# First modulation of a two-layer trunk: its last quarter of 512 channels computed as two parts of 256

## Chip, cores and metric

The kernel runs on one core of a Trainium2 chip. The metric is the device time of one execution in microseconds (us), as the median of several runs.

## The reference, cut to what matters

Two layers act on x, 256 tokens of 2048 channels. Each layer starts with a modulation: a vector c of 2048 values is multiplied with w_ada, and the shift and scale it gives are applied to the normalised x. The result h goes into one large product with w_in, whose columns feed three branches (a gated delta rule, a gated convolution, a sparse attention).

```python
cond = jax.nn.silu(c)
for layer in range(DEPTH):
    shift, scale, gate = jnp.split((cond @ w_ada[layer] + b_ada[layer])[:, None, :], 3, axis=-1)
    h = rms_norm(x, norm_g[layer]) * (1.0 + scale) + shift
    (qkv_a, z_a, beta_raw, alpha_raw, glu_in, z_b, q_c, k_c, v_c, z_c,
     q_i, k_i, w_i, gate_raw) = split_columns(h @ w_in[layer])
    ...
```

The change touches only layer 0's shift and scale, h, and the first three of the four groups of 512 columns of glu_in.

## The kernel before

**Layout.** Channels lie on the 128 partitions: 2048 channels are 16 tiles "kt" of 128, and a tile of h is 128 channels by 256 tokens. All is float32. Each product is made of three matmuls on rounded parts (high x high, high x low, low x high; function `three`, L940 to L942), so h exists as ah (high) and al (low), and a weight chunk as wh and wl.

**Weight chunks.** w_in comes in chunks of 2 kt by 512 columns (512 KB), through a ring of four slots. SyncE requests a chunk into raw once the chunk four before is split (`stream`, L394); ScalarE rounds it to wh once it has landed and TensorE has used the chunk four before (`rounds`, L560); GpSimd writes wl = raw - wh (L539); TensorE uses it in 2 x 4 x 3 = 24 matmuls and counts w_used. Below, "chunk n" is the n-th of these in the program.

**The first modulation.** To have h early, layer 0 computes shift and scale in four quarters of 512 channels. For a quarter, SyncE requests eight loads of w_ada (`ada_load`, L370; each is two transfers of 512 KB, for shift and for scale, two kt each), through four slots adaw. "Load n" counts them, 0 to 31; load n waits until load n - 4 is used (ada_used). VectorE adds up the 16 kt, one step of 128x1024 each, in `ada_part` (L1427, L1429), partly in PSUM and partly in acc. TensorE turns the totals onto partitions with one-column matmuls (`ada_sum`, L1029). VectorE makes mods and gsc of them (`quarter_mods`, L1483, L1487), then xs = merged * gsc + mods (L1526); ScalarE makes the high halves ah (`h_high`, L600), and VectorE the low ones (`h_low`, L1502), two kt at a time. Between these, VectorE adds the first steps of the next quarter (ADA_SIDE) and normalises x (L1412).

**The order of the work.** Every engine's order is written out by hand; semaphores join them. TensorE takes for each quarter the 4 kt of three column groups, called pairs 0, 1 and 2 (`part_gemm`), two chunks a pair, 24 chunks in all: chunks 18 to 23 belong to the last quarter. Each pair's PSUM keeps its sum through all quarters. Then it takes the fourth group (pair 3) with chunks 24 to 31, all 16 kt, and after that five more groups. SyncE mixes the chunks among the loads: chunks 18 to 23 are requested after load 31, then the masks (L361), eight skew stores (L430), then chunk 24 on. ScalarE casts chunk 18, makes h_high(3), and casts chunks 19 to 23. When the pairs are done, it copies pair 0 to glt (L623), takes the tanh of pair 1 (L548) and copies pair 2 to glt1 (L629); VectorE then starts the depthwise convolution (L1568, L1570).

The order in TensorE's block:

```python
for q in range(4):
    ada_sum(q)
    for pair in range(3):
        part_gemm(hc, pair, H, 4 * q, 4, G_IN, paired=pair == 0)
        hc += 2
part_gemm(hc, 3, H, 0, KT, G_IN)
```

## Time and profile before

| | us |
|---|---|
| median of 3 runs | 2204.05 (2202.7 to 2205.69) |
| the profiled execution, its own time | 2206.72 |
| its span in the profile | 2204.9 |
| TensorE busy, matmuls | 2140.4 (97%) |
| GpSimd busy | 1664.8 (76%) |
| VectorE busy | 1225.2 (56%) |
| ScalarE busy | 959.7 (44%) |

The profile is of one execution. A timeline row gives start, duration, engine, line, what is written from what, the form, how often, and in brackets the idle time before it with what ended it. Matmul ends are modelled: at the upper clock matmuls follow each other at 0.12 us although each is shown as 0.28. PE is TensorE, PEld its weight load, DVE VectorE, ACT ScalarE, POOL GpSimd, SP SyncE. PEclk is the granted TensorE clock as a share of 2.4 GHz.

### The profile page before, as it was taken

The page shows a single profiled execution, that of the slowest core. Times are in us where ns is not written, and L with a number is a line of the kernel's source. Part 1 is how long each engine was busy: PE and PEld are TensorE (multiplying, and loading weights), DVE is VectorE, ACT ScalarE, POOL GpSimd, SP SyncE. Part 2 cuts the span into 40 slices and gives each one's busy share as a digit, 9 for nine tenths or more (in the row PEclk, how much of TensorE's full clock was granted, in tenths as well). Part 3 has the DMA queues.
Part 4 walks back from the last instruction along what each step waited for, and adds up shares of the span by engine and source line. Part 5 has one row for each costly group of instructions (what it writes and reads, how often), then busy time and mean ns, then how long its engine had stood idle before and what let it go on. Part 6 is the DMA issues. An engine that isn't in the chain of part 4 may idle for free.

```text
span 2204.9 us, 37807 instructions
## 1 busy us (share of the span) xinstructions
PE 2140.4 (97%) x14842; PEld 1949.9 (88%) x14842; DVE 1225.2 (56%) x2153; ACT 959.7 (44%) x1056; POOL 1664.8 (76%) x676
## 2 busy tenths in 40 slices
PE   5799999999999999999989999999999999999999
PEld 3789999988879988788989999999788998888899
DVE  6859974847655455544562894756667455430110
ACT  3334444483333544444344344446633354444442
POOL 1558858767765898998868886877667679998876
PEclk7889999999999999999999999999999999999999
DMA  9978646545553699898975775555545458966754
GB/s 363 382 266 233 182 126 183 162 138 159 158 157 115 218 353 340 295 340 310 350 256 172 195 211 147 170 163 150 156 148 158 133 182 306 350 206 202 223 192 153
DMA packets 228987, 479.59 MB, mean 218 GB/s; under 512 B 22096, under 2 KB 26448, under 8 KB 220272
## 3 DMA queue, kind: packets, MB, share of 16 engines
q1 hardware_dynamic: 228688, 477.54, 67.1%
q8 instruction: 96, 1.57, 0.3%
q14 instruction: 43, 0.35, 0.0%
q10 hardware_dynamic: 160, 0.13, 0.0%
HBM read 471.19 MB, written 6.29 MB: 217 GB/s over the span
## 4 chain that ended last, share of the span: by engine, by line
PE 42%; POOL 30%; issue 23%; DVE 3%; ACT 1%; DVEq 1%; POOLq 0%; ACTq 0%
POOL wl L539 30%; PE ps L940 13%; PE ps L941 13%; PE ps L942 13%; DVE score L1632 1%; PE ps L1302 0%; ACT wh L560 0%; POOLq L538 0%; PE ps L1309 0%; PE ps L1290 0%; PE ps L1236 0%; ACTq L737 0%; PE ps L1225 0%; PE ps L1258 0%; PE ps L1252 0%
## 5 line engine op out<-in xcount | busy, mean ns | idle before, releaser
L539 POOL TENSOR_TENSOR wl<-raw,wh 128x1024 fp32r<-128x1024 f32 x672 | 1664.6, 2491 | 527.1 <-ACT wh L560 525.4
L560 ACT CAST wh<-raw 128x1024 fp32r<-128x1024 f32 x672 | 703.8, 1050 | 1118.2 <-PE ps L942 871.9
L940 PE MATMUL ps<-ah,wh 128*128 128x256 f32 x3008 | 867.7, 288 | 24.1 <-DVE al L1502 14.9
L941 PE MATMUL ps<-al,wh 128*128 128x256 f32 x3008 | 856.5, 285 | 0.0
L942 PE MATMUL ps<-ah,wl 128*128 128x256 f32 x3008 | 856.1, 285 | 0.0
L940 PEld LDWEIGHTS ps<-ah,wh 128*128 128x128 f32 x3008 | 583.0, 194 | 30.5 <-DVE al L1502 15.2
L941 PEld LDWEIGHTS ps<-al,wh 128*128 128x128 f32 x3008 | 583.2, 194 | 3.9 <-issue 3.6
L942 PEld LDWEIGHTS ps<-ah,wl 128*128 128x128 f32 x3008 | 582.8, 194 | 0.0
L940 PE MATMUL ps<-wh,ah 128*128 128x512 f32 (+1 forms) x832 | 319.8, 384 | 0.9 <-POOL wl L539 0.9
L942 PE MATMUL ps<-wh,al 128*128 128x512 f32 (+1 forms) x832 | 317.1, 381 | 0.0
L941 PE MATMUL ps<-wl,ah 128*128 128x512 f32 (+1 forms) x832 | 317.0, 381 | 0.0
L1570 DVE SCALAR_TENSOR_TENSOR ps<-upad,par,ps 128x256 f32<-128x256 f32 x480 | 199.7, 484 | 8.9
L940 PEld LDWEIGHTS ps<-wh,ah 128*128 128x128 f32 x832 | 156.5, 188 | 31.2 <-POOL wl L539 1.3
L942 PEld LDWEIGHTS ps<-wh,al 128*128 128x128 f32 x832 | 156.4, 188 | 30.4
L941 PEld LDWEIGHTS ps<-wl,ah 128*128 128x128 f32 x832 | 156.5, 188 | 28.9
L1448 DVE SCALAR_TENSOR_TENSOR ps<-modw,cond,ps 128x2048 f32<-128x2048 f32 x49 | 115.4, 2355 | 113.8 <-DMA modw<-w_ada 111.0
L940 PE MATMUL ps<-wh,yh 128*128 128x512 f32 x384 | 153.9, 401 | 0.0
L942 PE MATMUL ps<-wh,yl 128*128 128x512 f32 x384 | 149.8, 390 | 0.0
L941 PE MATMUL ps<-wl,yh 128*128 128x512 f32 x384 | 149.8, 390 | 0.0
L1736 DVE TENSOR_TENSOR ps<-ps,gbias 128x1024 f32<-128x1024 f32 x24 | 29.6, 1233 | 130.5 <-PE ps L942 130.5
L940 PEld LDWEIGHTS ps<-wh,yh 128*128 128x128 f32 x384 | 72.0, 188 | 16.1 <-POOL wl L539 0.7
L942 PEld LDWEIGHTS ps<-wh,yl 128*128 128x128 f32 x384 | 72.1, 188 | 15.5
(280 smaller groups left out, 1702.7 us busy)
## 6 DMA issues: line engine op xcount, KB each, us to landing
raw<-w_in SPq DMA_DIRECT2D x512, 512.0 KB, 3.7
modw<-w_ada SPq DMA_DIRECT2D x64, 1024.0 KB, 7.8
adaw<-w_ada SPq DMA_DIRECT2D x64, 512.0 KB, 8.5
raw<-w_out SPq DMA_DIRECT2D x64, 512.0 KB, 5.2
raw<-w_pc SPq DMA_DIRECT2D x32, 512.0 KB, 3.8
raw<-w_pb SPq DMA_DIRECT2D x32, 512.0 KB, 6.3
raw<-w_pa SPq DMA_DIRECT2D x32, 512.0 KB, 4.8
gbias<-b_gate SPq DMA_DIRECT2D x24, 256.0 KB, 4.3
```

The lines of the kernel that those rows point to most:

```text
L539: nc.gpsimd.tensor_tensor(wl[:, s], raw[:, s], wh[:, s].bitcast(F32), ALU.subtract).then_inc(sem("w_split"), 1)
L560: A.copy(wh[:, s], raw[:, s]).then_inc(sem("w_rounded"), 1)
L940: M.matmul(o, lh, rh, start=start, stop=False, skip_group_check=True)
L941: M.matmul(o, lh, rr, start=False, stop=False, skip_group_check=True)
L942: return M.matmul(o, ll, rh, start=False, stop=last, skip_group_check=True)
L1448: unit = V.scalar_tensor_tensor(o, w, cond[:, kt:kt + 1], wide if first < kt <= last else side, ALU.mult, ALU.add)
L1570: V.scalar_tensor_tensor(o, upad[:, ct, back:back + T], w, o, ALU.mult, ALU.add)
L1632: V.scalar_tensor_tensor(sc, rl[:, h, 0:keys], tok[:, qb, h:h + 1], sc, ALU.mult, ALU.add)
L1736: V.tensor_tensor(ps[:, 0:2, :], ps[:, 0:2, :], spread(gbias[:], 1, [P, TT, GW]), ALU.add).then_inc(sem("gate_sum"), 1)
```

## The change

The last quarter becomes two parts of 2 kt (256 channels). Each part has its own loads, totals, turning matmuls, mods, high and low halves, and its own three pieces of the pairs. So the program has five parts (ADA_PARTS).

- A load of the last quarter holds 4 kt by 256 columns instead of 2 kt by 512. Loads 24 to 27 are the first part's and 28 to 31 the second's. The bytes are the same; a contiguous row in memory is 1 KB instead of 2 KB.
- VectorE adds 16 steps of 128x512 for each part, up to the last step in one PSUM bank (pb[3]), with 3 steps of the first part and 4 of the second taken ahead (ADA_AHEAD).
- Chunks 18 to 23 come in another order: (pair 0, pair 1, pair 2) for kt 12 and 13, then the same for kt 14 and 15.
- TensorE turns the first part's totals ahead of pair 2 of the third quarter, and the second part's ahead of pair 2 of the first part.
- ScalarE casts chunks 18 and 19, makes the first part's high halves, casts 20 and 21, makes the second's, casts 22 and 23. Its copies of the pairs move by one or two casts.

```diff
         ADA_SIDE = 2
+        ADA_PARTS = ((0, 4), (4, 4), (8, 4), (12, 2), (14, 2))
+        ADA_AHEAD = (0, ADA_SIDE, ADA_SIDE, 3, 4)
         NORM = (2, 0, 1, 3)
...
+        def by_eighth(slot):
+            return adaw[slot][:].rearrange("p m s n -> p (m s n)").rearrange("p (m s n) -> p m s n", m=4, s=2)
         block = ctx.enter_context(nc.Block())
...
                 for part in (SHIFT, SCALE):
-                    col = part * D + q * GW
-                    sp.dma_start(adaw[j % 4][:, :, part], wa[0, :, 2 * j:2 * j + 2, col:col + GW]
-                                 ).then_inc(ada_landed[j % 4], 16)
+                    if q < 3:
+                        col = part * D + q * GW
+                        sp.dma_start(adaw[j % 4][:, :, part], wa[0, :, 2 * j:2 * j + 2, col:col + GW]
+                                     ).then_inc(ada_landed[j % 4], 16)
+                    else:
+                        col = part * D + 3 * GW + j // 4 * T
+                        sp.dma_start(by_eighth(j % 4)[:, :, part], wa[0, :, 4 * (j % 4):4 * (j % 4) + 4, col:col + T]
+                                     ).then_inc(ada_landed[j % 4], 16)
                 if n == 2:
...
-                    chunks = [(col, j) for q in range(4) for col in (first, second, first + GW)
-                              for j in range(2 * q, 2 * q + 2)]
+                    chunks = [(col, j) for k0, k in ADA_PARTS for col in (first, second, first + GW)
+                              for j in range(k0 // HK, (k0 + k) // HK)]
...
                     act.wait_ge(sem("gsc_ready"), q + 1)
-                    for kt in range(4 * q, 4 * q + 4):
+                    for kt in range(ADA_PARTS[q][0], sum(ADA_PARTS[q])):
                         last = A.activation(ah[:, kt], merged[:, kt], ACT.Identity, bias=mods[:, kt:kt + 1],
...
                         hc += 6
-                    rounds(hc, 1, hc % RING)
+                    rounds(hc, 2, hc % RING)
                     h_high(3)
-                    rounds(hc + 1, 5, (hc + 1) % RING)
+                    rounds(hc + 2, 2, (hc + 2) % RING)
+                    h_high(4)
+                    rounds(hc + 4, 2, (hc + 4) % RING)
                     hc += 6
-                    act.wait_ge(sem("w_used"), hc)
-                    A.copy(glt[:], pairv(0)).then_inc(gemm_free[0], 1)
                     rounds(hc, 2)
                     act.wait_ge(sem("w_used"), hc + 2)
+                    A.copy(glt[:], pairv(0)).then_inc(gemm_free[0], 1)
+                    rounds(hc + 2, 1, 2)
+                    act.wait_ge(sem("w_used"), hc + 3)
                     tanh_half(pairv(1), pairv(1)).then_inc(sem("glt_ready"), 1)
-                    rounds(hc + 2, 2, 2)
+                    rounds(hc + 3, 1, 3)
                     act.wait_ge(sem("w_used"), hc + RING)
...
                 for part in (SHIFT, SCALE):
-                    for j in range(4 * q, 4 * q + 4):
+                    for j in range(ADA_PARTS[q][0], sum(ADA_PARTS[q])):
                         mm = M.matmul(pb[2][:, part * KT + j:part * KT + j + 1], acc[:, part, j * P:(j + 1) * P],
...
                     pe.wait_ge(sem("bias_row"), HEADS)
-                    for q in range(4):
-                        ada_sum(q)
+                    for q, (k0, k) in enumerate(ADA_PARTS):
+                        if q < 3:
+                            ada_sum(q)
                         for pair in range(3):
-                            part_gemm(hc, pair, H, 4 * q, 4, G_IN, paired=pair == 0)
-                            hc += 2
+                            if q in (2, 3) and pair == 2:
+                                ada_sum(q + 1)
+                            part_gemm(hc, pair, H, k0, k, G_IN, paired=pair == 0)
+                            hc += k // HK
                     part_gemm(hc, 3, H, 0, KT, G_IN)
...
-                wide, side = ps[:, 6:8, :], acc[:, :, q * GW:(q + 1) * GW]
+                first, width = ADA_PARTS[q]
+                wide, side = ps[:, 6:8, :], acc[:, :, first * P:(first + width) * P]
+                if q > 2:
+                    wide = pb[3].rearrange("p (s n) -> p s n", s=2)
                 V.drain()
                 for kt in range(k0, k1):
-                    j, m = kt // 2, kt % 2
+                    j, m = kt // (8 // width), kt % (8 // width)
                     if m == 0:
-                        dve.wait_ge(ada_landed[j % 4], 32 * ((8 * q + j) // 4 + 1))
-                    w = adaw[j % 4][:, m]
-                    ahead = ADA_SIDE if q else 0
+                        dve.wait_ge(ada_landed[j % 4], 32 * ((first * 2 + j) // 4 + 1))
+                    w = by_eighth(j)[:, m] if q > 2 else adaw[j % 4][:, m]
+                    ahead = 0 if q > 2 else ADA_AHEAD[q]
                     o = wide if ahead <= kt < KT - 1 else side
...
                                                    ALU.mult, ALU.add)
-                    if m:
+                    if m == 8 // width - 1:
                         u.then_inc(sem("ada_used"), 1)
...
-                part = slice(4 * q, 4 * q + 4)
+                k0, k = ADA_PARTS[q]
                 dve.wait_ge(sem("ada_turned"), q + 1)
                 for n in (SHIFT, SCALE):
-                    at = n * KT + 4 * q
-                    last = V.tensor_tensor(mods[:, at:at + 4], pb[2][:, at:at + 4], p_(0, "b_ada", at, 4), ALU.add)
-                if q == 3:
+                    at = n * KT + k0
+                    last = V.tensor_tensor(mods[:, at:at + k], pb[2][:, at:at + k], p_(0, "b_ada", at, k), ALU.add)
+                if q == 4:
                     last.then_inc(sem("mods_ready"), 1)
                 V.drain()
-                V.scalar_tensor_tensor(gsc[:, part], mods[:, KT + 4 * q:KT + 4 * q + 4], 1.0,
-                                       p_(0, "norm_g", 4 * q, 4), ALU.add, ALU.mult)
+                V.scalar_tensor_tensor(gsc[:, k0:k0 + k], mods[:, KT + k0:KT + k0 + k], 1.0,
+                                       p_(0, "norm_g", k0, k), ALU.add, ALU.mult)
                 done("gsc_ready")
...
                 if layer == 0:
-                    for q in range(4):
+                    for q, (k0, k) in enumerate(ADA_PARTS):
                         if q == 0:
...
                             normed_x()
-                        normed_quarter(q)
-                        ada_part(q, ADA_SIDE + 1 if q else 10, KT)
+                        if q < 4:
+                            normed_quarter(q)
+                        ada_part(q, ADA_AHEAD[q] + 1 if q else 10, KT)
                         if q == 0:
...
                             dve.wait_ge(sem("con_landed"), 16)
-                        if q < 3:
-                            ada_part(q + 1, 0, ADA_SIDE)
+                        if q < 4:
+                            ada_part(q + 1, 0, ADA_AHEAD[q + 1])
                         quarter_mods(q)
-                        for kt in range(4 * q, 4 * q + 4):
+                        for kt in range(k0, k0 + k):
                             V.tensor_scalar(xs[:, kt], merged[:, kt], gsc[:, kt:kt + 1], mods[:, kt:kt + 1],
...
                         V.drain()
-                        h_low(2 * q)
-                        h_low(2 * q + 1)
-                        if q < 3:
-                            ada_part(q + 1, ADA_SIDE, ADA_SIDE + 1)
+                        for n in range(k0 // 2, (k0 + k) // 2):
+                            h_low(n)
+                        if q < 4:
+                            ada_part(q + 1, ADA_AHEAD[q + 1], ADA_AHEAD[q + 1] + 1)
```

How the instructions move. ScalarE, from the cast of chunk 16 (slot 0; the number behind raw_landed is the chunk's number modulo 4) to the glt copy, before:

```order
L560 CAST wh<-raw 128x1024 [waits w_used,raw_landed0]
L560 CAST wh<-raw 128x1024 [waits w_used,raw_landed1]
L560 CAST wh<-raw 128x1024 [waits w_used,raw_landed2]
L600 ACTIVATE ah<-merged,mods,gsc 128x256 [waits gsc_ready]
L600 ACTIVATE ah<-merged,mods,gsc 128x256 x3
L560 CAST wh<-raw 128x1024 [waits w_used,raw_landed3]
L560 CAST wh<-raw 128x1024 [waits w_used,raw_landed0]
L560 CAST wh<-raw 128x1024 [waits w_used,raw_landed1]
L560 CAST wh<-raw 128x1024 [waits w_used,raw_landed2]
L560 CAST wh<-raw 128x1024 [waits w_used,raw_landed3]
L623 COPY glt<-ps 128x1024 [waits w_used]
```

and in the change:

```order
L571 CAST wh<-raw 128x1024 [waits w_used,raw_landed0]
L571 CAST wh<-raw 128x1024 [waits w_used,raw_landed1]
L571 CAST wh<-raw 128x1024 [waits w_used,raw_landed2]
L571 CAST wh<-raw 128x1024 [waits w_used,raw_landed3]
L611 ACTIVATE ah<-merged,mods,gsc 128x256 [waits gsc_ready]
L611 ACTIVATE ah<-merged,mods,gsc 128x256
L571 CAST wh<-raw 128x1024 [waits w_used,raw_landed0]
L571 CAST wh<-raw 128x1024 [waits w_used,raw_landed1]
L611 ACTIVATE ah<-merged,mods,gsc 128x256 [waits gsc_ready]
L611 ACTIVATE ah<-merged,mods,gsc 128x256
L571 CAST wh<-raw 128x1024 [waits w_used,raw_landed2]
L571 CAST wh<-raw 128x1024 [waits w_used,raw_landed3]
```

The high halves of the last quarter (L600, now L611) stood behind chunk 18's cast and ahead of chunk 19's; now the first part's two stand behind chunk 19's cast, and the second part's two behind chunk 21's.

TensorE, at the turning of the last quarter's totals (ps<-con,acc), before:

```order
L942 MATMUL ps<-ah,wl 128x256
L940 MATMUL ps<-ah,wh 128x256
L941 MATMUL ps<-al,wh 128x256
L942 MATMUL ps<-ah,wl 128x256
L1029 MATMUL ps<-con,acc 128x1 [waits ada_summed]
L1029 MATMUL ps<-con,acc 128x1 x7
L940 MATMUL ps<-ah,wh 128x256 [waits w_split,hT_ready]
L941 MATMUL ps<-al,wh 128x256
```

and in the change, at the turning of the first part's, between pairs 1 and 2 of the third quarter:

```order
L956 MATMUL ps<-ah,wl 128x256
L954 MATMUL ps<-ah,wh 128x256
L955 MATMUL ps<-al,wh 128x256
L956 MATMUL ps<-ah,wl 128x256
L1043 MATMUL ps<-con,acc 128x1 [waits ada_summed]
L1043 MATMUL ps<-con,acc 128x1 x3
L954 MATMUL ps<-ah,wh 128x256 [waits w_split]
L955 MATMUL ps<-al,wh 128x256
```

The turning stood between two quarters, ahead of a matmul that waits for hT_ready too; now four matmuls of it (the rows count a turning matmul once; the trace has two records for each) stand ahead of pair 2, inside the third quarter. Those of the second part stand in the same way inside the first part, with 96 other matmuls between the two places.

## Rows read from the trace of the kernel before

**Rows 1.** The page, busy time, share and instructions of each engine.

```profile
PE 2140.4 (97%) x14842; PEld 1949.9 (88%) x14842; DVE 1225.2 (56%) x2153; ACT 959.7 (44%) x1056; POOL 1664.8 (76%) x676
```

**Rows 2.** Waits, whole run: us in total, times, longest us.

```profile
PE ps L940 <- POOL wl L539: 4.8, 4, 2.3
```

**Rows 3.** Timeline, TensorE, start, us, line, then idle before and releaser.

```profile
129.99 2.16 PE L1029 MATMUL ps<-con,acc 128*128 128x1 f32 x16 [1.15 <-DVEq L1433]
135.01 0.58 PE L940 MATMUL ps<-ah,wh 128*128 128x256 f32 x1 [2.86 <-DVE al L1502]
...
153.75 0.28 PE L942 MATMUL ps<-ah,wl 128*128 128x256 f32 x1
155.30 0.39 PE L940 MATMUL ps<-ah,wh 128*128 128x256 f32 x1 [1.28 <-POOL wl L539]
```

**Rows 4.** Timeline, ScalarE, 127 to 144 us.

```profile
127.51 1.05 ACT L560 CAST wh<-raw 128x1024 fp32r<-128x1024 f32 x1 [9.04 <-DMA raw<-w_in]
132.75 2.07 ACT L600 ACTIVATE ah<-merged,mods,gsc 128x256 fp32r<-128x256 f32 x4 [4.18 <-DVEq L1385]
134.72 2.92 ACT L560 CAST wh<-raw 128x1024 fp32r<-128x1024 f32 x3
139.72 1.05 ACT L560 CAST wh<-raw 128x1024 fp32r<-128x1024 f32 x1 [2.07 <-PE ps L942]
142.60 1.05 ACT L560 CAST wh<-raw 128x1024 fp32r<-128x1024 f32 x1 [1.83 <-PE ps L942]
```

**Rows 5.** Busy us by stretch (PE, PEld, DVE, ACT, POOL), PEclk, DMA share, GB/s.

```profile
136.00:138.00 2.00, 2.00 (x12) 2.00 (x11) 0.00 (x0) 1.65 (x2) 2.00 (x1) 0.50 0.00 0
```

**Rows 6.** SyncE's requests in its timeline, and the first four of the six.

```profile
101.85 17.97 SPq L370 DMA_DIRECT2D adaw<-w_ada  x10
119.86 18.75 SPq L394 DMA_DIRECT2D raw<-w_in  x6
...
145.07 37.55 SPq L394 DMA_DIRECT2D raw<-w_in  x16
...
L394 SPq DMA_DIRECT2D raw<-w_in x4: 467/508/1504, 119.9 to 121.5; - x4
...
DMA to landing us min/median/max: 7.6/8.8/9.9
```

**Rows 7.** Timeline, VectorE, 103 to 136 us.

```profile
103.37 1.20 DVE L1427 TENSOR_SCALAR acc<-adaw,cond 128x1024 f32<-128x1024 f32 x1 [1.54 <-DMA adaw<-w_ada]
...
106.02 0.23 DVE L1483 TENSOR_TENSOR mods<-ps,par 128x4 f32<-128x4 f32 x2
...
109.46 1.29 DVE L1429 SCALAR_TENSOR_TENSOR ps<-adaw,cond,acc 128x1024 f32<-128x1024 f32 x1
...
112.13 16.40 DVE L1429 SCALAR_TENSOR_TENSOR ps<-adaw,cond,ps 128x1024 f32<-128x1024 f32 x12
128.61 1.28 DVE L1429 SCALAR_TENSOR_TENSOR acc<-adaw,cond,ps 128x1024 f32<-128x1024 f32 x1
132.19 0.23 DVE L1483 TENSOR_TENSOR mods<-ps,par 128x4 f32<-128x4 f32 x2 [2.30 <-PE ps L1029]
...
134.26 1.30 DVE L1502 TENSOR_TENSOR al<-xs,ah 128x512 fp32r<-128x512 f32 x2
```

**Rows 8.** Groups by form, VectorE, 40 to 280 us: count, busy us, mean ns.

```profile
L1570 DVE SCALAR_TENSOR_TENSOR ps<-upad,par,ps 128x256 f32<-128x256 f32 x240 | 99.8, 484 | 4.5
L1429 DVE SCALAR_TENSOR_TENSOR ps<-adaw,cond,ps 128x1024 f32<-128x1024 f32 x38 | 49.0, 1290 | 5.0 <-DMA adaw<-w_ada 2.1
```

**Rows 9.** Stretch 106 to 108 us; GB/s in 40 slices of 206.5 to 214 us.

```profile
106.00:108.00 2.00, 0.00 (x0) 0.00 (x0) 1.78 (x7) 1.44 (x3) 0.00 (x0) 0.50 1.05 387
...
GB/s 142 66 98 175 295 360 371 393 415 301 257 229 240 221 227 246 216 224 194 276 355 344 355 366 363 328 344 325 259 306 300 273 360 295 355 328 344 355 355 453
```

**Rows 10.** Timelines of VectorE and TensorE about 275 us.

```profile
273.05 1.66 DVE L1576 TENSOR_SCALAR ub<-ps,par 128x256 f32<-128x256 f32 x4
...
277.82 3.33 PE L1100 MATMUL ps<-con,sqk 128*128 128x1 f32 x29
```

## The prediction, made before the changed kernel ran

> **What bounds the kernel now.** I read the busy shares first: TensorE is busy 97% of a span of 2204.9 us [rows 1], so time can only be gained or lost where it stands still or runs at half its clock. Over the whole run its waits for split weights come to 4.8 us in four places [rows 2]; nearly all else that stops it lies in the first 156 us, where the modulation is summed. From 155.30 us on, the work is paced by TensorE, at 2.88 us a weight chunk of 24 matmuls (two casts that each waited for a finished chunk start 2.88 us apart [rows 4]). So I ask one question: **when does TensorE start chunk 24**, the first one that belongs to no part. Before, this is 155.30 us [rows 3]. What that start moves, the end moves.
>
> The timeline of TensorE says what stands ahead of it. Its work on the third quarter ends 1.15 us before 129.99, at 128.84. It turns eight columns of totals (16 records, 2.16 us), waits for VectorE's al until 135.01, then runs the six chunks 18 to 23 without a hole until 153.87, and waits 1.3 us for chunk 24, which was requested late [rows 3, 6]. The restart is slow: the cast that waits for chunk 18 starts at 139.72, so that chunk took 4.7 us instead of 2.88. The granted clock is 0.50 (1.2 GHz) at 136 to 138 us [rows 5]. A restart after this hole costs about 1.8 us.
>
> VectorE's timeline shows why al came at 135: from 112.13 to 128.61 it adds twelve steps back to back, 1.37 us each, waiting for no transfer [rows 7]. SyncE's rows show that the six chunks 18 to 23 are requested behind the last modulation load, from 119.86 on, and that the first four of them land 7.6 to 9.9 us after their requests at 119.9 to 121.5 [rows 6]. Chunk 18 therefore lands at 127.5 (its cast starts at 127.51 [rows 4]), chunk 21 at 121.5 + 9.9 = 131.4, and chunk 19, at an even pace of 1.3 us, at 128.8.
>
> **The change part by part.**
>
> *Steps of VectorE.* The last quarter's 16 steps of 1024 elements become 32 of 512. A step of this form takes 484 ns at 256 elements and 1290 at 1024 [rows 8]; a straight line gives 753 at 512. With the 0.08 us that stands between two steps now (16.40 / 12 = 1.37 against 1.29 [rows 7]) one is 0.83 us. The quarter costs 32 x 0.83 = 26.6 us of VectorE instead of 16 x 1.37 = 21.9. The least it could be is half of 1.37, 0.68.
>
> *First part (channels 12 x 128 on).* Its first steps wait for the same load as before, to 103.37 [rows 7]. Three steps end at 105.9, so the third quarter's al is finished at 109.4 as before. One step, the normalisation (1.3) and twelve steps of 0.83 follow: the sum stands at 121.3. Four steps ahead for the second part reach 124.6. TensorE now turns these totals between pairs 1 and 2 of the third quarter. The last two chunks (48 matmuls) take 5.8 us, so pair 1 is done at 128.84 - 5.8 = 123.1: no wait there, and four columns instead of eight cost half of 2.16, about 1.1 us. The third quarter ends at about 129.9 instead of 128.84; mods and gsc of the first part stand at 125.1.
>
> *ScalarE in between.* Here the written order bites. Before, ScalarE cast one chunk (18) ahead of h_high of the last quarter; now it casts two, 18 and 19. So the first part's high halves wait for chunk 19's landing, h_low waits for them, and behind h_low stand all twelve steps left of the second part. Chunk 19 landed at 128.8. It now comes later for two reasons. SyncE requests load 31 when the fourth load of the quarter is used up, at 121.3 instead of 118.9; the transfers were queued until then, so I put 0.5 us on that. And each row of the quarter's loads is 1 KB instead of 2 KB. These are 16 transfers of 512 KB, 8.4 MB, which at 387 GB/s [rows 9] take 21.7 us. The nearest rows with short pieces are the bias load: where it moves 512-byte pieces it gets 194 to 246 GB/s, then with 1 KB pieces mostly 325 to 366 [rows 9]. Those sources start at odd addresses, these do not, so I take 360 GB/s, between 335 and 387: 23.3 us, 1.6 more. The ends are 0 and 3.3. Chunk 19 lands at 128.8 + 0.5 + 1.6 = 130.9.
>
> The Trainium skill ("DMA: Bandwidth & Descriptors", Specifications) gives 512 bytes as the least piece for full rate; by it the 1.6 us would be 0, but the 512-byte stretch at 227 GB/s does not agree. The same page ("Why small descriptors are slow (HBM only)") has a fixed 3 cycles a packet beside one per 32 bytes, which by my estimate is 70 against 67 cycles for 2 KB, about 1.0 us here.
>
> Then: cast 19 (1.05) to 131.95, two activations (half of the 2.07 us that four take) to 133.0, one h_low (0.65) to 133.7.
>
> *TensorE, first part.* It starts at 133.7 rather than 135.01: 1.3 us earlier. Chunk 18's split is there (cast 1.05 and split 2.4 after landing). It has stood for 3.8 us, so I charge one restart. Chunks 18 and 19 take 5.8 + 1.8, to 141.3.
>
> *The new wait.* TensorE may not go on with chunk 20: ada_sum of the second part now stands ahead of pair 2 and waits for the total. That is 133.7 + 12 x 0.83 = 143.7. So TensorE stands still for 2.4 us, with two thirds of the last quarter queued behind. The turning takes it to 144.8. Does the clock fall again? A hole of 1.28 us left it up; the hole before 135, with the turning inside it, did not. With the turning this one is 3.5 us. I take a second restart, 1.8 us, as likelier than not and keep 0 as the other end. Chunks 20 to 23 then end at 144.8 + 11.5 + 1.8 = 158.1. The second part's al (gsc 0.6, activations 1.05, h_low 0.65 and gaps after 144.8) is there at 147.4, before chunk 21 is due at 149.5; it hides.
>
> *Chunk 24.* SyncE can request it earlier than at 145.07, because chunk 19 is split earlier; the 1.3 us wait for it goes, already counted in the 158.1. It starts there: 158.1 - 155.3 = **2.8 us later**.
>
> *Edits that I cost at nothing.* The earlier requests of the eight skew stores are covered by TensorE's chunks 18 to 23. ScalarE's copies of the finished groups move behind other casts, but the depthwise convolution that they release has room: its last output is written at 274.7, and TensorE asks for it at 277.82 [rows 10]. Without that 3 us margin, their shift would count in full. One extra quarter_mods and its drains (0.6 us) lie ahead of h_low, in the time that ScalarE waits for chunk 19.
>
> **Sum.** 2.8 us against the profiled execution (2206.72 us, its span 2204.9) is 2209.5; the median of the runs lies 2.7 us below that execution, so I forecast 2204.05 + 2.8 = 2206.9 us. I count 0.2% (4.4 us) as what a measurement of this kernel tells from no change: the forecast is "within".
>
> **Rivals.**
> *A. The second restart does not come* (TensorE's hole is 2.4 us; 1.28 us did no harm, a longer one did). All else as above: 1.0 us, 2205.1 us.
> *B. Short rows are really slow* (ends slower). The modulation loads and all chunks behind them share the queue. If 1 KB rows move at the 227 GB/s of the bias load's short pieces, 8.4 MB take 37 us, 15.3 more; chunk 19, h_low, the second part's steps and chunk 24 all move: the forecast's 1.2 without rate loss and 15.3 make 16.5 us, 2220.6. It decides from a rate of about 337 GB/s down (24.9 us for the 8.4 MB, 3.2 more than now, 4.4 in all). Against it: more than half of the 1 KB stretch of the bias load is above that.
> *C. The overlap works as drawn.* If h_high did not have to wait for chunk 19, h_low would end at 126.9, the second sum at 136.9, and TensorE would start with chunk 18's split at about 131.4, after a hole of 1.5 us. Without a restart it has done chunks 18 and 19 by 137.2, the turning ends at 138.0, and it reaches chunk 24 at 149.5: 5.8 us saved, 2198.3 us. Against it: chunk 19 is requested behind load 31 in one queue, and nothing in the change moves it forward.
> That the change does not do what it says I rule out: the order shows the two parts.
>
> **How the numbers follow.** Forecast with both restarts 0.54, A 0.28, B and its milder forms beyond 4.4 us 0.14, C 0.04. The range: downwards full rate (-1.6), no second restart (-1.8) and steps at 0.68 us (-1.8) from 2206.9 give 2201.7; upwards 335 GB/s (+1.7) and transfers that run dry between two loads (+1.5, my guess: load 31's request now comes 2.4 us later) give 2210.1. Faster by over 0.2%: C, 0.04. Within: 0.82. Slower: B, 0.14.
>
> **What would show it.** In the changed profile: VectorE's 128x512 steps near 0.75 us; chunk 19's cast at 131 and the activations right behind it; h_low at 133 to 134; a TensorE wait of 2 to 3 us at its one-column matmuls near 144; half clock at 134 to 138 and again around 145; chunk 24 at 157 to 159. I am wrong if h_low of the first part ends before 129 (no wait for chunk 19), if chunks 19 to 21 land after 135 (slow rows), or if TensorE never stops between chunks 18 and 23.

## The result and the profile after

The changed kernel takes 2211.09 us (median of 7, 2206.69 to 2213.83), beside 2205.69 us (2201.85 to 2207.35) for the kernel before on the same chip: a ratio of 1.0027, interval 1.0014 to 1.0040, or 5.4 us more. Three more comparisons of the same two kernels, below, give 1.0009, 1.0019 and 1.0013. The mean of the four is 1.0017, 3.7 us. (A ratio is not the quotient of the two medians; the two differ by up to 1.6 us, in r1.) The forecast said 2.8 us more and 2206.9 us; the time lies outside its range, which ended at 2210.1.

The profiled execution took 2207.46 us, its span 2205.7. It is the second fastest of the seven and 3.6 us under their median. The page, against [rows 1]:

```profile
PE 2140.9 (97%) x14842; PEld 1949.9 (88%) x14842; DVE 1230.1 (56%) x2172; ACT 959.8 (44%) x1056; POOL 1662.9 (75%) x676
...
DMA packets 233083, 479.59 MB, mean 217 GB/s; under 512 B 22096, under 2 KB 34640, under 8 KB 224368
```

TensorE has as much to do as before. VectorE has 4.9 us more (26.6 - 21.9 = 4.7 were worked out). The packets under 2 KB were 26448 before: the 8192 more are the rows of 1 KB. No engine's total explains the time; it lies in when things start. TensorE's timeline, against [rows 3]:

```profile
131.94 0.38 PE L954 MATMUL ps<-ah,wh 128*128 128x256 f32 x1 [3.87 <-DVE al L1522]
...
142.04 1.19 PE L1043 MATMUL ps<-con,acc 128*128 128x1 f32 x8 [2.60 <-DVEq L1453]
```

Chunk 18 starts 3.1 us sooner than the 135.01 of before, 1.1 of it because this execution's third quarter was early (see below). Then the new wait stands where the forecast put it: 2.60 us for the second part's total. VectorE's timeline, against [rows 7]:

```profile
123.98 0.23 DVE L1503 TENSOR_TENSOR mods<-ps,par 128x2 f32<-128x2 f32 x2
124.29 0.16 DVE L1507 SCALAR_TENSOR_TENSOR gsc<-mods,par 128x2 f32<-128x2 f32 x1
124.57 0.73 DVE L1547 TENSOR_SCALAR xs<-merged,gsc,mods 128x256 f32<-128x256 f32 x2
131.19 0.69 DVE L1522 TENSOR_TENSOR al<-xs,ah 128x512 fp32r<-128x512 f32 x1 [5.89 <-ACT ah L611]
131.98 9.14 DVE L1449 SCALAR_TENSOR_TENSOR ps<-adaw,cond,ps 128x512 f32<-128x512 f32 x11
141.19 0.75 DVE L1449 SCALAR_TENSOR_TENSOR acc<-adaw,cond,ps 128x512 f32<-128x512 f32 x1
```

The first part is ready in VectorE at 125.3, but h_low waits 5.89 us for ScalarE's ah, and twelve steps of 0.83 us stand behind it. ScalarE's timeline, against [rows 4], says what held ah:

```profile
127.78 1.05 ACT L571 CAST wh<-raw 128x1024 fp32r<-128x1024 f32 x1 [10.98 <-DMA raw<-w_in]
129.12 1.04 ACT L571 CAST wh<-raw 128x1024 fp32r<-128x1024 f32 x1 [0.29 <-DMA raw<-w_in]
130.07 1.09 ACT L611 ACTIVATE ah<-merged,mods,gsc 128x256 fp32r<-128x256 f32 x2
```

The casts of chunks 18 and 19 both wait for transfers, and the two activations, ready since 124.5, stand behind them. Stretches of time (engines as in [rows 5], then PEclk, DMA share, GB/s) show the clock and, in the first row, the rate of the loads:

```profile
104.00:108.00 4.00, 0.24 (x1) 0.24 (x2) 3.57 (x11) 2.07 (x4) 0.00 (x0) 0.50 1.08 359
...
132.00:134.00 2.00, 2.00 (x12) 2.00 (x13) 1.80 (x3) 1.04 (x2) 2.00 (x1) 0.64 0.81 256
134.00:136.00 2.00, 2.00 (x11) 2.00 (x11) 1.83 (x3) 0.00 (x0) 2.00 (x2) 0.50 0.45 90
...
144.00:146.00 2.00, 2.00 (x11) 2.00 (x10) 1.56 (x4) 2.00 (x4) 0.08 (x1) 0.50 1.04 346
```

TensorE runs at the lower level (0.50, 1.2 GHz) after each of its two holes (the times in which it stands still). The loads with rows of 1 KB move 359 GB/s where 2 KB rows moved 387 [rows 9].

**One distance for all kernels.** Executions differ by a microsecond before the last quarter begins. So I measure from VectorE's mods of the third quarter (106.02 before [rows 7]; 104.96 after) to ScalarE's cast of chunk 32, which starts when chunk 28 is used. By then every kernel runs at 2.88 us a chunk, and this cast is 14.6 to 14.8 us after the start of chunk 24, the place that the forecast spoke of (155.30 before, 156.06 after). In ScalarE's timeline before:

```profile
170.05 1.05 ACT L560 CAST wh<-raw 128x1024 fp32r<-128x1024 f32 x1 [1.83 <-PE ps L942]
```

and after, VectorE's row and then ScalarE's:

```profile
104.96 0.23 DVE L1503 TENSOR_TENSOR mods<-ps,par 128x4 f32<-128x4 f32 x2
```

```profile
170.71 1.05 ACT L571 CAST wh<-raw 128x1024 fp32r<-128x1024 f32 x1 [1.83 <-PE ps L956]
```

The **distance** is 170.05 - 106.02 = 64.03 before, and 170.71 - 104.96 = 65.75 after: 1.7 us later in this execution (1.8 if counted to the start of chunk 24 itself). The forecast was 2.8.

### The profile page after: what moved, and what is told of

Its sections match the earlier page's. It is cut to its first block, busy times and chain, and to the rows that moved or that the text cites. A ratio compares the mean times of both kernels' runs of the same rounds, so it can differ in the third digit from the quotient of the medians.

```text
span 2205.7 us, 37848 instructions
## 1 busy us (share of the span) xinstructions
PE 2140.9 (97%) x14842; PEld 1949.9 (88%) x14842; DVE 1230.1 (56%) x2172; ACT 959.8 (44%) x1056; POOL 1662.9 (75%) x676
## 4 chain that ended last, share of the span: by engine, by line
PE 42%; POOL 31%; issue 22%; DVE 3%; ACT 1%; DVEq 1%; POOLq 0%; ACTq 0%; DMA 0%
POOL wl L550 31%; PE ps L954 13%; PE ps L955 13%; PE ps L956 13%; DVE score L1653 1%; ACT wh L571 0%; PE ps L1319 0%; POOLq L549 0%; PE ps L1326 0%; PE ps L1307 0%; PE ps L1253 0%; ACTq L751 0%; PE ps L1242 0%; PE ps L1275 0%; PE ps L1269 0%
```

## The experiments

All ran with rounds of the kernel before beside them on the same chip. "h_low" is the duration of VectorE's first-part al (in undivided kernels, that of four kt). "Hole 1" is TensorE's wait ahead of chunk 18, "hole 2" that at the second part's turning matmuls (in the undivided kernels at the whole quarter's). The ratio is to the kernel before, with its 95% interval; h_low, holes and distance are those of one profiled execution. A hole that the table leaves out stands ahead of chunk 24 where its transfer landed late: 1.28 us before, 2.01 in r1, 0.53 in r11, 1.34 in r9, and 2.46 us in r4 ahead of chunk 21.

| kernel | ratio (interval) | h_low | hole 1 | hole 2 | distance |
|---|---|---|---|---|---|
| before, profile above | 1 | 1.30 | 2.86 | 1.15 | 64.03 |
| r1 before again | 1.0002 (0.9991 to 1.0014) | 1.29 | 2.85 | 1.22 | 64.75 |
| change, profile above | 1.0027 (1.0014 to 1.0040) | 0.69 | 3.87 | 2.60 | 65.75 |
| r2 change again | 1.0009 (0.9996 to 1.0022) | 2.88 | 6.27 | 1.67 | 68.49 |
| r8 change, third | 1.0019 (1.0008 to 1.0029) | 2.89 | 6.52 | 1.82 | 68.66 |
| r14 change, fourth | 1.0013 (1.0001 to 1.0025) | 2.89 | 6.84 | 1.96 | 68.97 |
| r4 turning later | 1.0009 (0.9997 to 1.0022) | 0.69 | 4.60 | none | 66.79 |
| r7 one cast ahead | 1.0006 (0.9996 to 1.0015) | 1.95 | 3.88 | 1.95 | 66.43 |
| r12 activations divided | 1.0008 (0.9998 to 1.0018) | 1.00 | 3.40 | 4.07 | 66.76 |
| r13 activations delayed | 1.0027 (1.0013 to 1.0041) | 2.22 | 6.17 | 1.52 | 67.06 |
| r5 chunks 18, 19 requested early | 0.9992 (0.9979 to 1.0005) | 0.69 | none | 4.09 | 63.05 |
| r6 the same, undivided | 1.0007 (0.9998 to 1.0016) | 1.29 | 2.85 | 3.11 | 65.27 |
| r11 h_high first, undivided | 1.0015 (1.0002 to 1.0028) | 1.29 | 6.18 | 1.21 | 66.62 |
| r3 h_high first | 0.9987 (0.9975 to 0.9998) | 0.69 | 3.62 | none | 61.63 |
| r9 h_high first, again | 0.9995 (0.9980 to 1.0010) | 0.69 | 3.35 | none | 61.35 |
| r10 h_high first and early | 0.9981 (0.9966 to 0.9995) | 0.69 | 0.76 | 1.33 | 58.69 |

### First set: is it the order on ScalarE, or the place of the turning?

**r1, the kernel before unchanged.**

> The kernel before, unchanged, timed as if it were a change. Both theories: ratio 1.000, 2203 to 2207 us. Its mean granted clock run by run is the yardstick: theory K (the surplus beyond the 1 to 2 us that the trace of the change shows is extra time of TensorE at half clock after the two holes) expects these runs close together, near 0.985; theory R (the transfers of the last quarter differ from run to run) expects nothing of the clock.

Measured: 2210.38 us against 2208.36. Its profile has a span of 2214.1 us, 9 us more than the first profile of the same kernel, with chunk 24 at 155.12. So the span behind chunk 24 isn't constant: 2204.9 - 155.3 = 2049.6 in the first profile, 2059 here. Of the 16 profiles of this study eleven have 2049 to 2052 us there, four 2055 to 2059, one 2045.8, whatever the kernel. That spread is larger than the effect; the distance is the sharper measure.

The granted clock goes with it. Behind chunk 24, leaving out the last 5 us, it was at 0.50 for 10.2 us in the first profile (near 282 and 1149 us) and for 27.2 us in r1 (near 281, 1073, 1155 and 1352 us). At half the clock half of the 17 us between them is lost: 8.5 of the 9.4 us, an estimate. The other three long profiles have 20.4 us each; but so have r2 and r5, with 2050 and 2052, so it is not the whole account.

**r2, the change unchanged.**

> The change, unchanged, to see its spread again: the first profile has span 2205.7 at mean clock 0.987 while most of its timed runs had 0.983 and 2209 to 2212. Theory K: again slow runs (2209 to 2212 us) have the lower mean clock (0.983 or 0.984) and fast runs the higher; if the profile falls on a slow one, chunk 24 still starts at 155 to 160 us and the half clock lasts longer at chunks 18 and 20 (up to 3 us lost at each instead of 1.7), or later in the program. Theory R: chunk 19 lands at 133 or later in a slow run and chunk 24 starts after 159, the clock unchanged.

Measured: 2211.74 us, 3.4 above the kernel before (2.0 by the ratio, whose interval holds 1). The distance is 68.49, 2.7 us more than in the first profile. Late transfers made 0.5 of it: chunk 19's cast comes 24.71 us after mods(2), not 24.16. VectorE's timeline of r2 and then GpSimd's:

```profile
132.86 2.88 DVE L1522 TENSOR_TENSOR al<-xs,ah 128x512 fp32r<-128x512 f32 x1 [6.44 <-ACT ah L611]
135.85 2.46 DVE L1449 SCALAR_TENSOR_TENSOR ps<-adaw,cond,ps 128x512 f32<-128x512 f32 x3
```

```profile
130.55 9.76 POOL L550 TENSOR_TENSOR wl<-raw,wh 128x1024 fp32r<-128x1024 f32 x4 [9.80 <-ACT wh L571]
```

The same h_low that took 0.69 us takes 2.88, while GpSimd splits chunks 18 to 21 back to back, 2.35 us each. The steps behind it, and TensorE's chunk 18, move by the 2.2 us. In all three later profiles of the change (r2, r8, r14) the same two terms make up the distance: the cast of chunk 19 is 0.55, 0.75 and 1.04 us later than in the first, h_low 2.2 us longer, and the distance 2.74, 2.91 and 3.22 us more. The clock is lower for longer too (0.50 from 134 to 141 us in r2, from 132 to 135 in the first profile), but behind it TensorE still waits 1.67 us for the second total, so that is not what set chunk 24.

**r3, h_high(3) ahead of both casts.**

```diff
-                    rounds(hc, 2, hc % RING)
                     h_high(3)
-                    rounds(hc + 2, 2, (hc + 2) % RING)
+                    rounds(hc, 4, hc % RING)
                     h_high(4)
```

> The change, but ScalarE makes the first part's high halves ahead of the casts of chunks 18 and 19. Theory W (the wait for chunk 19 holds h_low, the second part's steps and so TensorE): h_low ends near 127, the second total stands near 137, TensorE starts chunk 18 when it is split (131) and is not stopped at chunk 20 or by under 1 us; chunk 24 starts at 150 to 152 instead of 156.3, 4 to 6 us faster than the change. Rival (the loads of the second part bind VectorE, landing at 124 to 128): the second total no earlier than 139, gain at most 2 us.

Measured: 2205.44 us against 2208.36, 6.3 us below the change beside it and 2.9 below the kernel before. ScalarE's and then TensorE's timeline:

```profile
124.50 1.09 ACT L611 ACTIVATE ah<-merged,mods,gsc 128x256 fp32r<-128x256 f32 x2 [7.15 <-DVEq L1401]
```

```profile
132.23 0.36 PE L953 MATMUL ps<-ah,wh 128*128 128x256 f32 x1 [3.62 <-POOL wl L550]
...
139.53 0.95 PE L1042 MATMUL ps<-con,acc 128*128 128x1 f32 x8
```

Chunk 18 starts no sooner than in the change (now the late chunk itself holds it), but the second total is there at 136.4 instead of 141.9, so hole 2 is gone. The change lost by one line of ScalarE's order: with it moved, h_low neither waits for chunk 19 nor falls on a split.

**r4, the second part's turning behind its pair 2.**

```diff
-                            if q in (2, 3) and pair == 2:
-                                ada_sum(q + 1)
+                            if q == 2 and pair == 2:
+                                ada_sum(3)
                             part_gemm(hc, pair, H, k0, k, G_IN, paired=pair == 0)
                             hc += k // HK
+                        if q == 3:
+                            ada_sum(4)
```

> The change, but the second part's totals are turned after pair 2 of the first part. TensorE then does three chunks before its hole. If the hole itself costs (theory: order of waiting only), it moves behind chunk 20: total at 141.9, turned at once, al at 145.6, chunk 21 then instead of at 147.3 minus one chunk: chunk 24 near 155.5 to 156.5, within 1 us of the change. If the clock is the cost (theory K), the hole is as long or longer (141 to 145.6) and the time is the same as the change, within 0.1%. A gain of over 2 us would speak for the hole's place as the cause of the surplus.

Measured: 2209.84, 1.9 us below the change beside it (the ratios are equal), but with h_low at 0.69 in this profile where the change had 2.88. Against the first profile of the change the distance is 1.0 longer, and chunk 19's cast came 1.3 us later (25.48 after mods(2), not 24.16); this accounts for it. The wait for the total turns into a 2.46 us wait for al behind the turning. No cost or gain of the turning's place shows; the wait moves and stays.

### Second set: late chunks, or the division?

**r5, the change, with chunks 18 and 19 requested behind load 29.**

```diff
+                        if n == 29:
+                            chunk(18)
+                            chunk(19)
-                    for i in range(18, 24):
+                    for i in range(20, 24):
```

> The change, with one thing moved: SyncE requests chunks 18 and 19 behind load 29 instead of load 31. Theory W (the change loses because ScalarE, ahead of the first part's high halves, waits for chunk 19 behind all loads): the casts of 18 and 19 fall before 125, h_low ends near 126.5, TensorE goes from the third quarter to chunk 18 with a hole under 1.5 us and no half clock, the second total stands at 136.4, and chunk 24 starts at 149 (151 if the clock falls at the second hole): 5 to 8 us faster than the change and 3 to 6 faster than before. Rival (the loads of the second part, now later by two chunks, 2.7 us, bind VectorE): idle time before its 128x512 steps, second total at 139 or later, gain under 3 us against the change.

Measured: 2206.23 us, 1.5 below the kernel before, with an interval that holds 1. The casts come at 121.37 and 122.99, so h_high isn't held by a transfer. But now the splits run while VectorE makes xs. VectorE's timeline of r5 and then GpSimd's:

```profile
124.36 0.56 DVE L1510 SCALAR_TENSOR_TENSOR gsc<-mods,par 128x2 f32<-128x2 f32 x1
125.04 2.70 DVE L1550 TENSOR_SCALAR xs<-merged,gsc,mods 128x256 f32<-128x256 f32 x2
127.81 0.69 DVE L1525 TENSOR_TENSOR al<-xs,ah 128x512 fp32r<-128x512 f32 x1
128.60 9.14 DVE L1452 SCALAR_TENSOR_TENSOR ps<-adaw,cond,ps 128x512 f32<-128x512 f32 x11
```

```profile
122.50 4.77 POOL L553 TENSOR_TENSOR wl<-raw,wh 128x1024 fp32r<-128x1024 f32 x2 [2.80 <-ACT wh L574]
```

The two xs instructions take 2.70 us instead of 0.73 and end 0.5 us behind the second split's end (122.50 + 4.77 = 127.27). That is the loss of r2 on another instruction. gsc (two operands in SBUF) took 0.56 us instead of 0.16 just ahead of it. The steps keep their 0.83 us beside the splits.

**r6, the kernel before, with the same early requests and both chunks cast ahead of h_high(3).**

> The kernel before, undivided, with the same early request of chunks 18 and 19 and both cast ahead of h_high(3). Theory W: what the division could save is the time between the sum of part 1 and of part 2; the request alone saves the 1.3 to 2 us wait for chunk 24 and no more, since al of the whole quarter comes at 135 as before: 0 to 2 us faster than before. Rival (the order of the requests is the whole gain, the division nothing): as fast as the early request with the division, 3 us or more under before.

Measured: 2208.84, 1.1 above the kernel before. In this form early chunks alone, without the division, gain nothing: the sum of the quarter comes later (mods at 29.15 us after mods(2), 26.17 before), and TensorE waits 3.11 us for the total and then turns it at half clock (3.58 us instead of 2.16).

**r7, one cast ahead of h_high(3) instead of two.**

```diff
-                    rounds(hc, 2, hc % RING)
+                    rounds(hc, 1, hc % RING)
                     h_high(3)
-                    rounds(hc + 2, 2, (hc + 2) % RING)
+                    rounds(hc + 1, 3, (hc + 1) % RING)
```

> The change, with the first part's high halves between the casts of chunks 18 and 19. Theory W: they wait for chunk 18's landing only, 1.35 us less than in the change: h_low and the second total 1.0 to 1.3 us earlier, chunk 24 1 us earlier, 1 us faster than the change, slower than with the high halves first. Theory K (clock only): no difference to the change. A h_low of over 2 us length, if it shows, falls beside GpSimd's split of chunk 18 or 19, as in the second profile of the change (2.88 us instead of 0.69).

Measured: 2208.79, 1.0 us above the kernel before, between the change and r3. h_low stands ready at 131.54, 0.95 us behind the start of chunk 18's split (130.59), and takes 1.95: it ends 2.90 us behind that start.

**r8, the change, a third time.**

> The change again, on the same chip as the others, for a third profile. Theory W and K together: chunk 24 between 156 and 161, time 2 to 4 us above before. If h_low of the first part is long again (2 to 3 us) it stands beside a GpSimd split; if it is short, chunk 24 starts before 158.

Measured: 2211.38, 3.6 us above the kernel before; h_low took 2.89 us again, and chunk 24 started at 158.93, not before 158.

### Third set: does h_high first hold, and what beats both?

**r9, r3 once more.**

> The change with h_high(3) ahead of both casts, once more. Theory (the end of the first modulation sets the time; the change loses by ScalarE's order and by h_low falling on a GpSimd split, and gains once both are gone): chunk 24 starts about 47.2 us after quarter 2's modulation (mods(2)), h_low of the first part takes 0.69 us, and the time is 2 to 3 us under the kernel before. Rival (the 2.9 us of its first run were a draw of the chip's clock elsewhere in the kernel): chunk 24 still 2 us earlier than before's 49.3 to 50.0, but the median within 1 us of the kernel before.

Measured: 2206.42 against 2207.94. Distance 61.35 and h_low 0.69, as expected; the median is 1.5 us under the kernel before, with an interval that holds 1, so the time by itself is inconclusive. Both runs together speak for a gain of about 2 us. The clock stayed at 1.00 through hole 1 this time; but chunk 24 landed late, and TensorE stood 1.34 us ahead of it.

**r10, r3 and the early requests of r5 together.**

> The change with h_high(3) ahead of both casts and chunks 18 and 19 requested right behind load 29. Theory: both chunks lie in SBUF by about 124, so their casts follow h_high(3) at once (125.5), the split of chunk 18 ends at about 128.5 to 129 instead of 132.2, TensorE goes from chunk 17 to 18 with a hole under 1.5 us, and then waits for the second part's total (136.4 to 137.5, loads a little later) 2 to 3 us; chunk 24 at 46 to 47 after mods(2), so 0 to 1 us under the kernel with h_high first alone, 3 to 4 under the kernel before. The steps of VectorE read one SBUF operand and one in PSUM and stay at 0.75 to 0.83 beside the splits; xs and h_low of the first part run before the first split and stay at 0.74 and 0.69. Rival (the second total is what bounds the end, whenever chunk 18 starts): the hole moves ahead of ada_sum whole, and the time is that of h_high first alone within 0.5 us, or above it by the half clock after two holes.

Measured: 2203.69 against 2207.94, 0.9981 (0.9966 to 0.9995). The timelines of r10, VectorE and TensorE:

```profile
124.61 0.74 DVE L1549 TENSOR_SCALAR xs<-merged,gsc,mods 128x256 f32<-128x256 f32 x2
125.68 0.69 DVE L1524 TENSOR_TENSOR al<-xs,ah 128x512 fp32r<-128x512 f32 x1 [0.33 <-ACT ah L614]
126.46 9.14 DVE L1451 SCALAR_TENSOR_TENSOR ps<-adaw,cond,ps 128x512 f32<-128x512 f32 x11
```

```profile
129.20 0.36 PE L956 MATMUL ps<-ah,wh 128*128 128x256 f32 x1 [0.76 <-POOL wl L553]
...
136.52 1.05 PE L1045 MATMUL ps<-con,acc 128*128 128x1 f32 x8 [1.33 <-DVEq L1455]
```

Holes of 0.76 and 1.33 us instead of 3.87 and 2.60, and the clock stays at 1.00 through both. Distance 58.69, 5.3 us under the 64.03 of before. Chunk 24 starts 44.0 us after mods(2), where 46 to 47 were expected: the gain was put too low. Against r3 a restart is gone (r3 ran at 0.50 from 134 to 137), against r9 the late chunk 24. By this one comparison, whose interval ends just under 1, it beats the kernel before by 4.3 us, and by about 8 the change (4.3 + 3.7; the two were not measured side by side).

**r11, the kernel before with h_high(3) ahead of the cast of chunk 18.**

```diff
-                    rounds(hc, 1, hc % RING)
                     h_high(3)
-                    rounds(hc + 1, 5, (hc + 1) % RING)
+                    rounds(hc, 6, hc % RING)
```

> The kernel before, its last quarter undivided, with h_high(3) ahead of the cast of chunk 18. Theory (the order pays only with the quarter divided): the total of the whole quarter comes at about 132, h_high to 133.6, so the cast of chunk 18 and its split come only then (split to about 136.5) and TensorE starts chunk 18 at 136.5 to 137 instead of 134.3 to 135.0; of these 2 us the 1.3 to 2.0 us wait for chunk 24 hides most: the time 0 to 1.5 us over the kernel before. Rival (the gain of h_high first came from the order alone and not from the division): 2 to 3 us under the kernel before.

Measured: 2211.37, 3.4 us above the kernel before (0 to 1.5 expected: right in sign, too small; the longer restart came on top, chunk 18 starting at 137.34). The order alone loses; it gains only with the quarter divided.

### Fourth set: is h_low's length a toss?

By now h_low's start lay behind the start of chunk 18's split by 131.19 - 128.90 = 2.29 us in the change's first profile and 2.29 in r4 (short both times), and by 2.31 in r2 and 2.30 in r8 (long both times). The split ends after 2.35. GpSimd's rows of the change's first profile:

```profile
128.90 2.35 POOL L550 TENSOR_TENSOR wl<-raw,wh 128x1024 fp32r<-128x1024 f32 x1 [9.61 <-ACT wh L571]
...
131.21 2.92 POOL L550 TENSOR_TENSOR wl<-raw,wh 128x1024 fp32r<-128x1024 f32 x1
```

The second split's row starts 0.02 us behind h_low's (131.19), and this split takes 2.92 us instead of 2.35: here GpSimd is the one that waits. In r2 it starts 0.01 us ahead of h_low's, and takes 2.34.

**r12, the part's two activations on either side of the cast of chunk 19.**

```diff
-                def h_high(q):
+                def h_high(q, k0=0, k1=9):
...
-                    for kt in range(ADA_PARTS[q][0], sum(ADA_PARTS[q])):
+                    for kt in list(range(ADA_PARTS[q][0], sum(ADA_PARTS[q])))[k0:k1]:
...
-                    rounds(hc, 2, hc % RING)
-                    h_high(3)
+                    rounds(hc, 1, hc % RING)
+                    h_high(3, 0, 1)
+                    rounds(hc + 1, 1, (hc + 1) % RING)
+                    h_high(3, 1, 2)
```

> The change with the first part's two activations divided about the cast of chunk 19 (one ahead of it, one behind), so that both are done 0.5 us sooner after the cast of chunk 18, everything else in its place. Theory of the toss (in four profiles h_low stood ready 2.29, 2.31, 2.30 and about 2.3 us behind the start of chunk 18's split, which lasts 2.35: twice it got VectorE's turn and took 0.69 us, twice the split of chunk 19 came first and it took 2.9): now h_low stands ready about 1.8 us behind the split's start, waits 0.55 us for its end and is served ahead of the next split: it takes 1.1 to 1.3 us each time, ends 3.0 to 3.1 us after the split's start, TensorE starts chunk 18 at about 27.0 after mods(2), and the cast of chunk 32 comes at 65.7 to 66.0 after it, as in the change's own lucky profile; 1 to 2 us under the change's median. Rival (h_low is long for a reason of its own, or the waiting engine has no precedence): it takes 2.9 to 3.4 us in this profile and the time is the change's.

The timelines of r12, VectorE and GpSimd:

```profile
131.28 1.00 DVE L1524 TENSOR_TENSOR al<-xs,ah 128x512 fp32r<-128x512 f32 x1 [5.69 <-ACT ah L611]
```

```profile
129.38 9.86 POOL L550 TENSOR_TENSOR wl<-raw,wh 128x1024 fp32r<-128x1024 f32 x4 [9.23 <-ACT wh L571]
```

h_low is ready 1.90 us behind the split's start, ends 2.90 behind it, and TensorE starts chunk 18 at 27.08 after mods(2), as expected (27.0). So an instruction that already waits is served ahead of the next split, which then takes 2.85 us (2.83 in r7). The distance is 66.76, not the expected 65.7 to 66.0. Hole 1, 3.40 us, left the clock up, so chunks 18 and 19 were done sooner; hole 2 grew to 4.07, the clock fell inside it, at 141, and the turning ran at the lower level (1.86 us instead of 1.19). The median is 2210.1, 2.7 us over the kernel before (the interval of the ratio holds 1) and 1.7 us under r14's.

**r13, the first activation done twice**, with a drain behind it, so that h_low is ready half a microsecond later.

```diff
                     rounds(hc, 2, hc % RING)
+                    h_high(3, 0, 1)
+                    A.drain()
                     h_high(3)
```

> The change with the first of the part's two activations done twice (the first result is overwritten by the same values), so that h_low stands ready 0.5 to 0.7 us later and always inside the split of chunk 19. Theory of the toss: h_low takes 2.3 to 2.6 us and ends with that split and 0.6 us on, at the same place as in the change's unlucky profiles: cast of chunk 32 at 68.5 to 68.8 after mods(2), about 4 us over the kernel before in every execution. Rival (no lock: a later h_high costs its own delay): h_low 0.69 us, cast of chunk 32 at 66.3, 0.5 us over the change's lucky profile.

The timelines of r13, VectorE and GpSimd:

```profile
133.15 2.22 DVE L1524 TENSOR_TENSOR al<-xs,ah 128x512 fp32r<-128x512 f32 x1 [7.18 <-ACT ah L611]
```

```profile
130.18 9.77 POOL L550 TENSOR_TENSOR wl<-raw,wh 128x1024 fp32r<-128x1024 f32 x4 [9.70 <-ACT wh L571]
```

It ends at 135.37, 5.19 us behind the first split's start. In r2, r8 and r14 it ends 5.19, 5.19 and 5.20 behind it. It was ready 0.66 us later than in r2 (2.97 against 2.31 us behind that start), and this delay is swallowed whole: h_low waits for the end of the second split, whenever it was ready within it. The median is 5.5 us over the kernel before. The distance, 67.06, misses the expected 68.5 to 68.8: chunk 18 started at 29.81 after mods(2), as in r2 (29.72), but this execution's second hole, 1.52 us, left the clock up, and the restart of 1.6 us did not come.

**r14, the change, a fourth time.**

> The change unchanged, beside the two. Theory of the toss: h_low takes either 0.69 or 2.9 us, the cast of chunk 32 is at 65.7 or 68.6 after mods(2), and the median lies between those of the two kernels above or at the one with the delay. Rival: a third value.

The timelines of r14, VectorE and GpSimd:

```profile
133.63 2.89 DVE L1522 TENSOR_TENSOR al<-xs,ah 128x512 fp32r<-128x512 f32 x1 [6.93 <-ACT ah L611]
```

```profile
131.32 7.42 POOL L550 TENSOR_TENSOR wl<-raw,wh 128x1024 fp32r<-128x1024 f32 x3 [10.37 <-ACT wh L571]
```

Ready 2.31 us behind the split's start, and long. Measured 2211.77, below r13 and above r12, as the theory has it. In five profiles of this order the two at 2.29 were short and the three at 2.30 and 2.31 long.

## Why the prediction was wrong, and what of it was right

The step that failed is a term of the sum: one h_low at 0.65 us, in the step on ScalarE. Three of the four profiles of the change show 2.88 and 2.89 us there. The path and the two waits came as forecast.

**Right: which place decides.** The start of chunk 24, here as the distance, goes with the ratios, if not in strict order. The four runs under 64 are the only ones with a ratio under 1; the largest ratios belong to the change (65.75 to 68.97) and to r11 and r13 (66.6 to 67.1). The change's first comparison fits least, with the largest ratio and the smallest distance of its four. r10 with 5 to 6 us less in its distance gained 4.3, the change with 3.6 us more (mean of its four profiles, 67.97, less 64.39, the mean of the two of before) lost 3.7.

**Right: VectorE's steps.** 0.75 us each and 0.83 from one to the next (9.14 / 11), as worked out from [rows 8].

**Right: ScalarE's order holds the first part.** r3 shows it by undoing it, and r11 that the order gains only with the quarter divided. Chunk 19's cast was forecast at 24.9 us after mods(2); it came at 24.16, 24.71, 24.91 and 25.20. The rate of 1 KB rows was taken as 360 GB/s; it is 359.

**Right: the new wait and the second restart.** The hole was forecast at 2.4 us; it was 2.60 in the profile with a short h_low. The clock fell after the second hole in all four profiles of the change. Rival A needed it to stay up, which only r13 and r10 show among the divided kernels that have this hole. The forecast had the first restart at 1.8 us too: chunks 18 and 19 took 7.50 us in the first profile, 1.7 more than at the upper level, and the wait for the total hid it. Rival B's slow rows did not come. Rival C, h_high not held by chunk 19, is what r3 built: it was priced at 5.8 us gained, and r3 and r9 gained 1 to 3, since chunk 18 itself still landed late (TensorE waited for its split until 132.23, not 131.4) and r3's restart came; r10, with the chunk early too, gained 4.3.

**Wrong: "one h_low (0.65)".** In the step on ScalarE I added h_low at its length of before, and priced nothing for the two engines side by side. Before, h_low fell between two splits: it ran from 134.26 [rows 7], while GpSimd's split of chunk 18 ended at 131.0 and the next began at 135.83:

```profile
128.64 2.35 POOL L539 TENSOR_TENSOR wl<-raw,wh 128x1024 fp32r<-128x1024 f32 x1 [7.70 <-ACT wh L560]
135.83 7.11 POOL L539 TENSOR_TENSOR wl<-raw,wh 128x1024 fp32r<-128x1024 f32 x3 [4.84 <-ACT wh L560]
```

In the change it stands 2.3 us behind the start of the first of four splits in a row, and three times in four it took 2.88 to 2.89 us instead of 0.69: 2.2 us more, in the chain that ends at chunk 24. With that term at 2.9, the forecast's own sum gives 158.1 + 2.2 = 160.3. Counted from the third quarter of before (mods at 106.02), chunk 24 starts at 159.9, 160.0 and 160.3 in r2, r8 and r14. In the profile with the short h_low it started at 156.06, 2.0 us sooner than forecast, 1.1 of which because that execution's third quarter was 1.1 us early. The low and high cases together, one in four and three in four, make a mean of 3.6 us over before, where 2.8 was said.

So the direction and most of the size were right (by the mean of four comparisons the change is within 0.2%; in the first it is just over, in the class that the forecast gave 0.14, for rival B's slow rows, which did not come). What failed was a range whose upper end held no term for VectorE beside GpSimd. The trace of before would have shown the need for such a term: there a 128x1024 TENSOR_SCALAR of the same loads, which takes 1.20 us in [rows 7], takes 2.44 here, and ends 0.55 us behind the split that it fell on (71.76 + 2.34 = 74.10). VectorE and GpSimd:

```profile
72.21 2.44 DVE L1427 TENSOR_SCALAR acc<-adaw,cond 128x1024 f32<-128x1024 f32 x1 [0.82 <-DMA adaw<-w_ada]
```

```profile
71.76 2.34 POOL L539 TENSOR_TENSOR wl<-raw,wh 128x1024 fp32r<-128x1024 f32 x1 [0.48 <-ACT wh L560]
```

How often h_low was long in the first comparison is not shown: its one profiled execution has the short one, and the other six were not profiled. Part of the miss is not the kernel's. The forecast was laid on a median of three runs of the kernel before, 2204.05; with four more it is 2205.69, 1.6 us higher, and the range was missed by 1.0. As a difference it reached to 6.1 us more (2210.1 - 2204.05), and 5.4 lies inside. And the ratio of this comparison, 1.0027, is the largest of four.

**Open.** Why the rest of the kernel, behind chunk 24, takes 2049 us in most executions and up to 2059 in some, beyond the part that goes with the granted clock (r1); and which holes let TensorE's clock fall. In the divided kernels it stayed up through a hole 1 of 0.76, 3.35 and 3.40 us and fell at or in those of 3.62 us and more; at hole 2 it stayed up at 1.33 and 1.52 and fell at 1.67 and more. What lies ahead of a hole seems to count too, and I did not separate it.

## What to carry to other kernels

When a stage is divided so that its first half starts early, list for each engine what is written ahead of that half's steps, and ask which of it waits for a transfer: two casts in front of two activations took the gain away, and moving them brought 5 to 6 us back (the mean ratio of r3 and r9, 0.9991, against the change's 1.0017). Before pricing a short VectorE instruction in a critical chain, look at what GpSimd does at that moment; one with both inputs in SBUF cost nearly a whole GpSimd instruction more here, and near the border of two of them that was a toss of 0.02 us. When two holes stood in series, closing one alone enlarged the other (r5, r12); the largest step came with both short and the clock up (r10).

## What the hardware showed that I had not expected

Some instructions of VectorE and GpSimd shut each other out for their whole length. h_low (two operands in SBUF) took 0.69 us with no split beside it, and 1.00, 1.95, 2.22 and 2.88 us when it became ready 1.90, 0.95, 2.97 and 2.31 us behind the start of the first of a row of 2.35 us splits: where it had to wait it ended 2.90 us behind that start, or 5.19 to 5.20. The split that came behind h_low took 2.82 to 2.92 us instead of 2.35. xs (one operand in SBUF, output in SBUF) took 2.70 us for its two instructions instead of 0.73. The steps, with one operand and often the result in PSUM, took 0.83 us beside splits as without.

The Trainium skill ("SBUF — State Buffer", Who interferes with whom) says this of h_low's case: the pair of ports that the two share is an exclusive lock, taken for the whole instruction by whichever starts first, and a VectorE instruction with two SBUF inputs contends for it with a GpSimd instruction that reads SBUF. By that rule and the 2.35 us of a split, an estimate for h_low is 0.69 to 3.0 us; the trace agrees, with 0.69 to 2.89. That sentence does not cover xs, which has one SBUF input. What the rows add is who comes next when one waits: in r12 and r7 the waiting h_low went ahead of GpSimd's next split, and at the border it turned on two starts that lie 0.02 us apart or less.

Loads in rows of 1 KB instead of 2 KB moved 359 instead of 387 GB/s in the change's first profile, 7% less.
